# Cross attention: scores in three one-pass products, remainders and the division of the weights on the pool engine

## The reference, cut to what matters

```python
def mem_xattn(h, mk, mv, wq, wo):
    b, t, _ = h.shape
    q = (h @ wq).reshape(b, t, XA_HEADS, XA_HEAD_DIM)
    s = jnp.einsum('bthd,bmhd->bhtm', q, mk).astype(jnp.float32) * (XA_HEAD_DIM ** -0.5)
    p = jax.nn.softmax(s, axis=-1).astype(mv.dtype)
    o = jnp.einsum('bhtm,bmhd->bthd', p, mv).reshape(b, t, XA_HEADS * XA_HEAD_DIM)
    return o @ wo
```

## Time and profile before

| | us |
|---|---|
| median of 3 runs | 2899.81 (2899.16 to 2900.58) |
| the profiled execution, its own time | 2901.42 |
| its span, from the first to the last instruction | 2899.7 |
| PE busy | 2729.0 (94%) |
| DVE busy | 1577.7 (54%) |
| ACT busy | 972.4 (34%) |
| POOL busy | 676.9 (23%) |
| TensorE's mean granted clock | 0.977 of full speed |

### The profile page before, as it was taken

How to read it: one execution, slowest core, us unless ns; L and a number is a source line. 1 busy time by engine, 2 the same in 40 slices (tenths; PEclk the granted TensorE clock), 3 DMA queues, 4 the chain that set the end, 5 groups by cost and what they waited for, 6 DMA issues and landing times. The chain is left out here.

```text
span 2899.7 us, 45445 instructions
## 1 busy us (share of the span) xinstructions
PE 2729.0 (94%) x16837; PEld 2336.5 (81%) x16837; DVE 1577.7 (54%) x2498; ACT 972.4 (34%) x1751; POOL 676.9 (23%) x624
## 2 busy tenths in 40 slices
PE   7999999978899899999989999999989999999988
PEld 7988888834354688899749999999967779999567
DVE  5367676787656667553334434333448973250634
ACT  5311111254565311232234322323334443231331
POOL 0001222222232132221002224422226622220020
PEclk9999999989999999999999999999999999999999
DMA  7477998787623821221664233323258875313741
GB/s 272 140 246 241 344 361 317 258 248 226 194 73 100 280 65 45 83 90 66 227 210 144 86 104 119 110 96 104 102 185 274 280 245 180 107 57 118 263 153 67
DMA packets 300159, 498.82 MB, mean 172 GB/s; under 512 B 45113, under 2 KB 175802, under 8 KB 299586
## 3 DMA queue, kind: packets, MB, share of 16 engines
q1 hardware_dynamic: 280642, 429.13, 44.8%
q0 software_dynamic: 15120, 51.46, 5.1%
q10 hardware_dynamic: 4176, 15.32, 1.3%
HBM read 383.06 MB, written 117.00 MB: 172 GB/s over the span
## 5 line engine op out<-in xcount | busy, mean ns | idle before, releaser
L905 PE MATMUL ps<-in_hi,w_halves 128*128 128x344 f32 x1536 | 498.4, 325 | 7.8 <-DVE in_lo L816 7.6
L907 PE MATMUL ps<-in_hi,w_halves 128*128 128x344 f32 x1536 | 492.3, 321 | 0.0
L906 PE MATMUL ps<-in_lo,w_halves 128*128 128x344 f32 x1536 | 491.8, 320 | 0.0
L663 POOL TENSOR_TENSOR w_halves<-w_raw,w_halves 128x1024 fp32r<-128x1024 f32 x60 | 146.6, 2447 | 685.4 <-ACT w_halves L736 685.3
L905 PEld LDWEIGHTS ps<-in_hi,w_halves 128*128 128x128 f32 x1536 | 290.5, 189 | 15.9 <-DVE in_lo L816 14.8
L906 PEld LDWEIGHTS ps<-in_lo,w_halves 128*128 128x128 f32 x1536 | 289.8, 189 | 1.8 <-issue 0.6
L907 PEld LDWEIGHTS ps<-in_hi,w_halves 128*128 128x128 f32 x1536 | 290.3, 189 | 0.0
L1954 PE MATMUL ps<-in_hi,wv_hi 128*128 128x344 f32 x696 | 229.3, 329 | 3.7 <-DVE wv_lo L1802 3.7
L1955 PE MATMUL ps<-in_lo,wv_hi 128*128 128x344 f32 x696 | 224.4, 322 | 0.0
L1956 PE MATMUL ps<-in_hi,wv_lo 128*128 128x344 f32 x696 | 224.4, 322 | 0.0
L503 PE MATMUL ps<-in_hi,w_halves 128*128 128x344 f32 x640 | 205.3, 321 | 1.8 <-DVE w_halves L378 1.8
(11 more groups left out here) (435 smaller groups left out, 6052.1 us busy)
## 6 DMA issues: line engine op xcount, KB each, us to landing
k_pages<-in_cache_k SPq DMA_DIRECT2D x256, 256.0 KB, 4.6
v_pages<-in_cache_v POOLq DMA_DIRECT2D x160, 256.0 KB, 5.5
v_pages<-in_cache_v SPq DMA_DIRECT2D x96, 256.0 KB, 3.0
w_raw<-in_w_c SPq DMA_DIRECT2D x48, 512.0 KB, 4.4
in_raw<-og SPq DMA_DIRECT2D x120, 172.0 KB, 3.4
cc<-residual SPq DMA_DIRECT2D x120, 172.0 KB, 1.8
kq_raw<-in_w_mem SPq DMA_DIRECT2D x32, 512.0 KB, 4.0
w_words<-in_mem_k SPq DMA_DIRECT2D x16, 1024.0 KB, 6.5
```

The source lines that it names most:

```text
L663: return eng.tensor_tensor(w_lo[:, m % KT, :], raw[:, m % RAW, :], w_hi[:, m % KT, :].bitcast(f32), ALU.subtract)
L905: pe.matmul(acc(n), w_hi[:, t, a:b], h, start=(kt == 0), stop=False)
L906: pe.matmul(acc(n), w_hi[:, t, a:b], l, start=False, stop=False)
L907: last = pe.matmul(acc(n), w_lo[:, t, a:b], h, start=False, stop=(kt == KT - 1))
```

## The change

The scores of batches 1 to 7 are formed from parts; batch 0 keeps the float32 products. ACT rounds the keys of a head (`keys_high`) and the queries of a batch (`queries_high`). POOL subtracts to get the remainders (`keys_low`, `queries_low`). `scores(n)` then has 24 one-pass products in place of 16 float32 instructions and waits for the remainders (`kk_lo_done`, `q_lo_done`). The product of the weights with the reciprocal of their sum moves from DVE to POOL (`normal`); DVE keeps the reciprocal. POOL's queue, in order: `keys_low(0)`, `queries_low(1)`, `normal(0)`, and then in each turn n `normal(n + 1)`, at a new head `keys_low`, and `queries_low(n + 2)`. The key and query buffers are given back to SP once their remainders are made. The new tiles take the room of an unused one (`gap`), so that nothing else moves.

```diff
--- before.py
+++ after.py
@@ -3006,13 +3006,17 @@
         smx, snmx, ssm, srs = (sb(n, [NR, 1]) for n in ("xs_mx", "xs_nmx", "xs_sum", "xs_rs"))
         spt = sb("xs_pt", [128, MB, S, NR + XH])
         om = sb("xs_masked", [2 * NR, HALF])
-        sb("gap", [128, 5452])
+        q_hi, q_lo = (sb(n, [128, 2, 2, BT], f32r) for n in ("xa_q_hi", "xa_q_lo"))
+        kk_hi, kk_lo = (sb(n, [128, 2, MEM], f32r) for n in ("xa_k_hi", "xa_k_lo"))
+        sb("gap", [128, 332])
         o, so = sb("xa_o", [128, 2, 2, BT]), sb("xs_o", [128, KT, S])
         cached_in = [sem(f"cached{j}") for j in range(NKV)]
         (q_in, rows_done, dot_done, zt_done, smx_done, snmx_done, se_done, srs_done, sp_done, st_done, spt_done,
-         pv_done, om_done, col_done, so_done, so_stored, zeroed, qt_done, sel_done, qr_hi_done, qr_lo_done) = (
+         pv_done, om_done, col_done, so_done, so_stored, zeroed, qt_done, sel_done, qr_hi_done, qr_lo_done,
+         kk_hi_done, kk_lo_done, q_hi_done, q_lo_done) = (
             sem(n) for n in ("q_in", "rows", "dot", "zt", "smx", "snmx", "se", "srs", "sp", "st", "spt", "pv", "om",
-                             "col", "so", "so_st", "zeroed", "qt", "sel", "qr_hi", "qr_lo"))
+                             "col", "so", "so_st", "zeroed", "qt", "sel", "qr_hi", "qr_lo",
+                             "k_hi", "k_lo", "q_hi", "q_lo"))
 
 
 
@@ -3021,6 +3025,12 @@
             if i < 2:
                 return k.cached_early[i], 16 * (layer + 1)
             return cached_in[i % NKV], 16 * (i // NKV + (i % NKV >= 2))
+
+        def queries_of(n):
+            return q[n // PER % 2][:, :, BT * (n % PER):BT * (n % PER) + BT]
+
+        def head_landed(eng, h):
+            eng.wait_ge(*((head_in[h % 2], 48 * (h // 2 + h % 2)) if h else (k.head0_in, 48 * (layer + 1))))
 
         block = ctx.enter_context(nc.Block())
 
@@ -3029,7 +3039,10 @@
             def head_keys(h):
                 u = h % 2
                 if h >= 2:
-                    sp.wait_ge(s_done, PER * (h - 1))
+                    sp.wait_ge(q_lo_done, PER * (h - 1) - 1)
+                    sp.wait_ge(kk_lo_done, h - 1)
+                    if h == 2:
+                        sp.wait_ge(s_done, 1)
                     sp.wait_ge(vt_done, h - 1)
                 for dst, src in ((kk, kv[kv0 + 2 * h:kv0 + 2 * h + 2]), (vt, kv[kv0 + 8 + 2 * h:kv0 + 8 + 2 * h + 2])):
                     sp.dma_start(dst[u], src.rearrange("t p n -> p t n")).then_inc(head_in[u], 16)
@@ -3077,20 +3090,26 @@
         @block.tensor
         def _(pe):
             def scores(n):
-                h = n // PER
-                if n % PER == 0:
-                    pe.wait_ge(*((head_in[h % 2], 48 * (h // 2 + h % 2)) if h else (k.head0_in, 48 * (layer + 1))))
-                if n >= 1:
+                if n == 0:
+                    head_landed(pe, 0)
+                else:
+                    pe.wait_ge(kk_lo_done, n // PER + 1)
+                    pe.wait_ge(q_lo_done, n)
                     pe.wait_ge(e_done, NB * n)
                 for b in range(NB):
-                    a = BT * (n % PER) + 128 * b
+                    z_out, a = ps[:, b // 2, MEM * (b % 2):MEM * (b % 2) + MEM], slice(128 * b, 128 * b + 128)
                     for j in range(2):
-                        last = pe.matmul(ps[:, b // 2, MEM * (b % 2):MEM * (b % 2) + MEM], q[h % 2][:, j, a:a + 128],
-                                         kk[h % 2][:, j, :], start=(j == 0), stop=(j == 1))
+                        if n == 0:
+                            last = pe.matmul(z_out, q[0][:, j, a], kk[0][:, j, :], start=(j == 0), stop=(j == 1))
+                            continue
+                        pe.matmul(z_out, q_hi[:, n % 2, j, a], kk_hi[:, j, :], start=(j == 0), stop=False)
+                        pe.matmul(z_out, q_hi[:, n % 2, j, a], kk_lo[:, j, :], start=False, stop=False)
+                        last = pe.matmul(z_out, q_lo[:, n % 2, j, a], kk_hi[:, j, :], start=False, stop=(j == 1))
                 last.then_inc(s_done, 1)
 
             def values(h):
                 if h >= 1:
+                    head_landed(pe, h)
                     pe.wait_ge(oc_done, PER * h - 1)
                 for m in range(MB):
                     for j in range(2):
@@ -3203,6 +3222,33 @@
             pe.wait_ge(e_done, NB * NBATCH)
             k.warm(pe, 1, 0)
 
+        @block.gpsimd
+        def _(pool):
+            def keys_low(h):
+                pool.wait_ge(kk_hi_done, h + 1)
+                pool.tensor_tensor(kk_lo[:, :, :], kk[h % 2], kk_hi[:, :, :].bitcast(f32), ALU.subtract).then_inc(kk_lo_done, 1)
+
+            def queries_low(n):
+                pool.wait_ge(q_hi_done, n)
+                pool.tensor_tensor(q_lo[:, n % 2], queries_of(n), q_hi[:, n % 2].bitcast(f32), ALU.subtract
+                                   ).then_inc(q_lo_done, 1)
+
+            def normal(n):
+                pool.wait_ge(rs_done, n + 1)
+                pool.tensor_tensor(p[:, n % 2], p[:, n % 2], rs[:, n % 2, :, None].broadcast_to((128, NB, MEM)),
+                                   ALU.mult).then_inc(p_done, 1)
+
+            keys_low(0)
+            queries_low(1)
+            normal(0)
+            for n in range(NBATCH):
+                if n + 1 < NBATCH:
+                    normal(n + 1)
+                if n + 2 < NBATCH:
+                    if (n + 2) % PER == 0:
+                        keys_low((n + 2) // PER)
+                    queries_low(n + 2)
+
         @block.vector
         def _(dve):
             def maxima(n):
@@ -3216,10 +3262,9 @@
 
             def weights(n):
                 dve.wait_ge(e_done, NB * (n + 1))
+                if n >= 2:
+                    dve.wait_ge(p_done, n - 1)
                 dve.reciprocal(rs[:, n % 2, :], sm[:, n % 2, :]).then_inc(rs_done, 1)
-                dve.wait_ge(rs_done, n + 1)
-                dve.tensor_tensor(p[:, n % 2], p[:, n % 2], rs[:, n % 2, :, None].broadcast_to((128, NB, MEM)),
-                                  ALU.mult).then_inc(p_done, 1)
 
             def dots(s):
                 dve.wait_ge(*page_in(s))
@@ -3281,6 +3326,17 @@
                                    bias=nmx[:, n % 2, b:b + 1], scale=SCALE,
                                    accum_out=sm[:, n % 2, b:b + 1]).then_inc(e_done, 1)
 
+            def keys_high(h):
+                head_landed(act, h)
+                if h:
+                    act.wait_ge(s_done, PER * h)
+                act.copy(kk_hi[:, :, :], kk[h % 2]).then_inc(kk_hi_done, 1)
+
+            def queries_high(n):
+                if n >= 3:
+                    act.wait_ge(s_done, n - 1)
+                act.copy(q_hi[:, n % 2], queries_of(n)).then_inc(q_hi_done, 1)
+
             def copy_out(n):
                 act.wait_ge(o_done, n + 1)
                 if n >= 2:
@@ -3300,6 +3356,8 @@
                              ).then_inc(spt_done, 1)
 
             act.copy(sel[:, :, :], k.c("ident")[0:S, 0:S, None].broadcast_to((S, S, 128))).then_inc(sel_done, 1)
+            keys_high(0)
+            queries_high(1)
             exponentials(0)
             for n in range(NBATCH):
                 if n >= 2:
@@ -3315,6 +3373,10 @@
                 beside(n, 0)
                 act.wait_ge(t_done, n + 1)
                 act.copy(pt[:, n % 2], ps[:, 2:4, :]).then_inc(pt_done, 1)
+                if n + 2 < NBATCH:
+                    if (n + 2) % PER == 0:
+                        keys_high((n + 2) // PER)
+                    queries_high(n + 2)
                 beside(n, 1)
                 beside(n, 2)
             copy_out(NBATCH - 2)
```

## The result

The changed kernel has a median of 2929.79 us (2923.20 to 2930.87); the kernel before, on the same chip, 2899.48 (2896.76 to 2900.58). The forecast was 2926.8. The profiled execution took 2929.76 us, of which the span is 2928.1: 28.4 more than the 2899.7 of before.

A forecast was written before the change was run, and what follows sets the result against it. PE bounds the kernel before; after the change a chain through softmax and POOL does. Full clock +16.2 us and clock falls +10.8 sum to +27.0 on 2899.8: 2926.8 us, range 2913 to 2943.

The forecast's parts named there:

- The bound passes from PE to a chain through POOL: Cross attentions: scores(n+1) wait for queries_low(n+1) behind normal(n), hence for batch n's softmax; 11.86 us, 13.14 with keys_low.
- POOL's prices: POOL's operations, from nearest rows: normal 1.90 us, queries_low 2.45, keys_low 1.28.
- The turns at full clock: Start of batch 1's scores to batch 7's: 76.75 us a stage, +9.41 and +7.96; +16.2 us in all.
- S(5) to S(6): Start of batch 5's scores to batch 6's: 13.33 us, samples' softmax ahead of the reciprocal; PE waits 3.7.
- The clock: PE's added waits bring three half-clock stretches a stage, at 1.8 us each: 10.8 us; bounds 0 to 23.
- What was costed at nothing: ACT's rounding hidden by 0.3 to 0.9 us; ACT's added waits, DVE's lost 1.22 us, SP's earlier release: no effect.
- Nothing changes outside the stages: Outside the two cross attention stages nothing changes; stages some 12 to 15 us longer.
- The sum: Full clock 16.2 us plus clock falls 10.8 make +27.0 on the median 2899.8: 2926.8 us.
- rival 3: The chain holds and the clock falls in every early turn at the upper price: 39.2 us, 2939; chance 17%.

The follow-up runs named there:

- e1: The changed kernel with keys_low and queries_low(n+2) put ahead of normal(n+1) in POOL's queue; 2916.04 us, 1.0054 of the kernel before.
- e2: e1 with ACT rounding queries of batch n+2 ahead of batch n+1's exponentials, and queries_low ahead of keys_low on POOL; 2898.66 us, 0.9995 of the kernel before.
- e6: The changed kernel with queries_low made twice on POOL for each batch; 2964.82 us, 1.0219 of the kernel before.
- e5: The changed kernel with unused constant products in PE's waits, in turn 0 and ahead of the scores of batches 2 to 6; 2915.99 us, 1.0054 of the kernel before.
- e4: The kernel before, float32 scores, with only the product of the weights moved from DVE to POOL; 2898.67 us, 0.9995 of the kernel before.
- e3: The changed kernel with the product of the weights back on DVE, POOL making only the remainders; 2918.66 us, 1.0057 of the kernel before.
- e8: e2 with SP asking for heads 2 and 3 a turn earlier, and three constant products in turn 0; 2892.05 us, 0.9973 of the kernel before.

## Why the prediction was right, step by step

- **The bound passes from PE to a chain through POOL.** Right: the waits of L3105, and e1, e2 and e6, which shortened, cut and lengthened the chain.
- **POOL's prices.** `normal` 1.89 us for 1.90, `queries_low` 2.35 for 2.45, `keys_low` 1.27 for 1.28. The nearest row of the same operation and shape on the same engine was as good as a measurement.
- **The turns at full clock.** 76.75 forecast, 76.20 in e5. From the reciprocal's start to POOL's there were 0.25 us (0.21 forecast), from POOL's end to PE's start 0.10; each turn is within 0.12 of its forecast. Against before the full clock part is +15.3 for +16.2.
- **S(5) to S(6).** Length right (13.21 for 13.33), place of the wait half wrong: the 3.7 us of the forecast came as 1.69 ahead of the samples' weighted values (L3181) and 1.74 ahead of the scores. Neither was followed by a fall.
- **The clock.** The term that was mis-sized twice, each way: six falls at 1.8 were put in, 10.8; there were five, and e5 puts them at 9.9, a full one at 2.3. The price taken was the lower of the two rows; the upper one, 5.95 - 3.62, was it. That 10.8 and 9.9 come so near is luck, and with another number of falls they would not. The places were half right: falls were forecast after the waits ahead of the scores of batches 2, 4 and 6. Those around the scores of batch 2 came in both stages, but behind the wait of turn 0; those of batch 4 came as forecast, those of batch 6 not at all, and one came at the scores of batch 3.
- **What was costed at nothing.** The rounding on ACT was hidden as said: in the turn shown it ended at 1456.71, before POOL had ended `normal` (1457.21). The product on POOL instead of DVE: e4, nothing.
- **Nothing changes outside the stages.** Wrong by 3.2 us: the first stage starts 1.7 later, 1.3 are won between the stages, 2.8 are lost after the second. The first two may be chance: over the ten profiled executions the first stage starts anywhere from 1404.98 to 1415.66 us, and 1173.6 to 1179.3 us lie between the stages. The 2.8 are not. From the second stage to the end pass 131.0 to 131.6 us in all eight kernels with one-pass scores, and 128.7 and 128.9 in the two with float32 scores (before, e4). The difference has its place in the last output projection, 83.5 us behind the stage, where PE waits for an input that a transfer brings: 1.98 and 1.89 us in those two, 2.35 to 2.99 in the eight, and in the eight alone a stretch at half clock follows. PE's first product behind that wait, before and after, and windows of what follows:

```profile
2856.50 0.42 PE L905 MATMUL ps<-in_hi,w_halves 128*128 128x344 f32 x1 [1.98 <-DVE in_lo L816]
2883.02 0.42 PE L905 MATMUL ps<-in_hi,w_halves 128*128 128x344 f32 x1 [2.84 <-DVE in_lo L816]
```

```profile
2857.00:2861.00 4.00, 4.00 (x27) 4.00 (x26) 1.68 (x4) 0.49 (x1) 0.00 (x0) 1.00 0.25 90
2883.40:2886.90 3.50, 3.50 (x15) 3.50 (x14) 1.39 (x4) 0.49 (x1) 0.00 (x0) 0.51 0.27 101
```

The longer wait is 0.9 us of the 2.8, the half clock some 1.5. Why that transfer comes later when the scores are one-pass, no run shows.

- **The sum.** 15.3 + 9.9 + 3.2 = 28.4 for 27.0. That it is off by 1.4 only is luck in part: two terms were 0.9 too high, and 3.2 stood at nothing. In the medians the loss is 30.3, and the 1.9 beyond the profiled execution are within what repeated runs show. (The range has a slip: its lower end by its own words is 2916.0 - 2 = 2914, not 2913.)

On the rule that carried rival 3 the runs now say more. The Trainium skill ("TensorE: Matmul & The Clock Gate", section "HAM oscillation — how this bites in real kernels") has a loop with a wait of some 3 to 5 us in each round fall back in every round. For waits of that length the trace agrees, and for shorter ones it goes either way. The ten waits ahead of the scores of batches 2 to 6 were 4.44, 1.30, 3.22, 1.12, 1.74 us in the first stage and 4.37, 1.25, 3.22, 1.19, 1.74 in the second. The two ahead of batch 2 can't be counted, since the clock fell before the one began and 0.6 us into the other. Of the other eight, both of 3.22 us and the one of 1.30 were followed by half clock or had it begin in them, and the five others not. In e6 the eight of that kind were 3.68 to 5.63 us, and all were. In e3 it came behind a wait of only 0.50 us, 0.8 us after PE had started again; two others of 0.50 us in that run had none. PE had been busy for 8.73 of the 8.80 us ahead of it:

```profile
1462.50:1471.30 8.80, 8.73 (x40) 5.23 (x39) 6.05 (x23) 4.79 (x11) 2.02 (x1) 1.00 1.04 353
1471.33:1471.83 0.50, 0.00 (x2) 0.03 (x1) 0.50 (x5) 0.46 (x1) 0.40 (x1) 1.00 0.96 328
1472.70:1476.00 3.30, 3.30 (x18) 3.30 (x17) 0.84 (x6) 0.00 (x0) 0.00 (x0) 0.50 0.51 150
```

So not every round falls back here, and what decides about the short waits is open.

## What to carry to other kernels

Before moving work to an idle engine, write that engine's queue out and ask of each entry who waits for it and what stands ahead: here a remainder that depended on loaded data alone stood behind a division that depended on the whole softmax, and so chained one batch to the next. An engine's low busy share (26% for POOL) says nothing of that; the sum along the chain does. Where PE comes to wait, add the clock to the wait, and when work is drawn forward, draw its transfers forward as well. And before calling the rest outside a changed stage chance, lay the same stretch of all runs side by side: here 2.8 us of 3.2 came back in every kernel with the new scores.

## What the runs showed of the hardware beyond that

- The half clock can come after a wait as short as 0.50 us (e3, ahead of 1471.83; 1.30 in the changed kernel, ahead of 1446.32), and end in the middle of the scores that follow. In the changed kernel the turn with the 1.30 us wait then took 1.5 us more than in e5, and those in which all 24 one-pass products ran at half clock 2.3. Constant products in the waits kept the clock at 1.00 in both stages of e5 and e8.
- POOL's subtraction of 512 elements took 1.54 to 1.79 us where it overlapped DVE's product of two operands in SBUF (e3), and 1.27 without (e1, with the same rounding on ACT beside it); DVE's 1.22 us did not change. The Trainium skill ("SBUF — State Buffer", section "Who interferes with whom") names just this pair, a DVE instruction with two inputs in SBUF and a POOL instruction that reads SBUF, as contending; by the trace they do, and it was POOL that paid. With the division on POOL as well, in e1, that overlap is gone, which is the 0.27 us of the turn M5 to M6.
